# One-column products in place of transposes for the modulation turns, and four waits behind means taken out

## The reference

```
silu_c = jax.nn.silu(c)                                   # [1, 2048]
mod_l = jnp.split(silu_c @ w_mod[l] + b_mod[l], 6, axis=-1)   # w_mod [2048, 12288]
hl  = modulate(rms_norm(xl, norm1_g[l]), mod_l[0], mod_l[1])
xl  = xl + mod_l[2][:, None, :] * mixer_output(...)
hl2 = modulate(rms_norm(xl, norm2_g[l]), mod_l[3], mod_l[4])
xl  = xl + mod_l[5][:, None, :] * sq_relu_ffn(hl2, ...)

# layer_norm, in the gated branch (sgu) and in the convolution branch
xc  = xf - jnp.mean(xf, axis=-1, keepdims=True)
var = jnp.mean(xc * xc, axis=-1, keepdims=True)
```

## Time and profile before

| | |
|---|---|
| median of 3 runs | 2732.12 us (2731.7 to 2733.49) |
| the profiled execution | 2731.7 us, span 2729.9 us |
| TensorE matmuls | 2675.9 us busy, 21400 |
| TensorE weight loads | 2556.2 us busy, 21400 |
| VectorE | 1914.7 us busy, 2949 instructions |
| ScalarE | 1268.8 us busy, 1836 instructions |
| DMA | 539.02 MB, mean 197 GB/s |

### The profile page before, as it was taken

One profiled execution on the slowest core, in us unless ns is written; L12 is line 12 of the kernel. 1 busy time (PEld: TensorE's weight loads), 2 busy tenths in 40 slices (PEclk: granted clock), 3 DMA queues, 4 the chain that ended last, 5 costly groups with the idle time before them and its releaser, 6 DMA issues.

```text
span 2729.9 us, 51382 instructions
## 1 busy us (share of the span) xinstructions
PE 2675.9 (98%) x21400; PEld 2556.2 (94%) x21400; DVE 1914.7 (70%) x2949; ACT 1268.8 (46%) x1836; POOL 149.9 (5%) x162
## 2 busy tenths in 40 slices
PE   7999999999999999999999999999999999989998
PEld 4599977899999999999999999999999999989997
DVE  5765789889897788886555555677656665478564
ACT  4622344454446445544443444464444444554453
POOL 0000011100014001100000000030000000100000
PEclk9999999999999999999999999999999999999999
DMA  7766755455555788887555565564434444535553
GB/s 302 300 226 232 236 179 180 143 200 186 186 187 185 250 287 276 268 279 245 185 187 189 182 195 189 188 195 151 159 132 155 154 147 147 174 125 190 184 194 131
DMA packets 163991, 539.02 MB, mean 197 GB/s; under 512 B 31024, under 2 KB 35120, under 8 KB 163632
## 3 DMA queue, kind: packets, MB, share of 16 engines
q1 hardware_dynamic: 163760, 535.73, 58.9%
HBM read 533.57 MB, written 2.10 MB: 196 GB/s over the span
## 4 chain that ended last, share of the span: by engine, by line
PE 88%; DVE 6%; DMA 3%; issue 1%; ACT 1%; SPq 1%; DVEq 0%; POOL 0%; ACTq 0%
PE ps L566 26%; PE ps L571 26%; PE ps L568 26%; DVE lo L1694 2%; DMA raw<-in_w_ff 2%; PE ps L782 1%; PE ps L801 1%; DMA raw<-in_w_mod 1%; PE ps L729 1%; PE ps L717 1%; PE ps L790 1%; ACT hi L1078 1%; DVE row L2269 1%; PE ps L959 0%; SPq L484 0%
## 5 line engine op out<-in xcount | busy, mean ns | idle before, releaser
L1078 ACT ACTIVATE hi<-raw 128x1024 fp32r<-128x1024 f32 x856 | 901.3, 1057 | 899.4 <-PE ps L571 477.1
L566 PE MATMUL ps<-AH,hi 128*128 128x256 f32 (+2 forms) x4432 | 1263.4, 285 | 2.8 <-DVE AL L2108 2.7
L571 PE MATMUL ps<-AH,lo 128*128 128x256 f32 (+2 forms) x4432 | 1252.0, 282 | 7.3 <-DVE lo L1694 7.3
L568 PE MATMUL ps<-AL,hi 128*128 128x256 f32 (+2 forms) x4432 | 1253.3, 283 | 0.0
L1694 DVE TENSOR_TENSOR lo<-raw,hi 128x1024 fp32r<-128x1024 f32 x856 | 1038.6, 1226 | 205.1 <-ACT hi L1078 203.6
L566 PEld LDWEIGHTS ps<-AH,hi 128*128 128x128 f32 x4432 | 837.4, 189 | 32.8 <-issue 29.1
L571 PEld LDWEIGHTS ps<-AH,lo 128*128 128x128 f32 x4432 | 836.2, 189 | 10.1 <-DVE lo L1694 10.0
L568 PEld LDWEIGHTS ps<-AL,hi 128*128 128x128 f32 x4432 | 835.4, 188 | 0.8
L571 PE MATMUL ps<-YH,lo 128*128 128x256 f32 (+1 forms) x1512 | 421.1, 279 | 0.6 <-DVE lo L1694 0.5
L566 PE MATMUL ps<-YH,hi 128*128 128x256 f32 (+1 forms) x1512 | 421.1, 279 | 0.0
L568 PE MATMUL ps<-YL,hi 128*128 128x256 f32 (+1 forms) x1512 | 421.1, 279 | 0.0
(11 more groups left out here) (277 smaller groups left out, 2491.5 us busy)
## 6 DMA issues: line engine op xcount, KB each, us to landing
raw<-in_w_ff SPq DMA_DIRECT2D x256, 512.0 KB, 4.2
raw<-in_w_in SPq DMA_DIRECT2D x208, 512.0 KB, 4.2
raw<-in_w_mod SPq DMA_DIRECT2D x192, 512.0 KB, 4.8
raw<-in_w_ain SPq DMA_DIRECT2D x128, 512.0 KB, 3.6
raw<-in_w_pin SPq DMA_DIRECT2D x64, 512.0 KB, 3.5
raw<-in_w_o SPq DMA_DIRECT2D x32, 512.0 KB, 4.7
raw<-in_w_aout SPq DMA_DIRECT2D x32, 512.0 KB, 3.5
raw<-in_w_pout SPq DMA_DIRECT2D x32, 512.0 KB, 3.5
```

The lines of the kernel that those rows point to most:

```text
L566: e.matmul(b.ap[:, o], hi[:, k, :], xh, start=start and k + i == 0, stop=False, skip_group_check=many)
L568: e.matmul(b.ap[:, o], hi[:, k, :], xl, start=False, stop=False, skip_group_check=many)
L571: mm = e.matmul(b.ap[:, o], los[j % NSPLIT][:, k, :], xh, start=False, stop=stop and k == KU - 1, skip_group_check=many)
L1078: e.activation(his[u % NSPLIT][:, :, :], raws[raw_at[i]][:, :].rearrange("p (k m) -> p k m", k=KU), ACT.Copy).then_inc(s_hi, 1)
```

## The change

Three edits. The turn on TensorE is four plain products in place of four transposes: the stationary operand is the same slice of `macc`, the moving operand is a column of ones (`one`, one number on each partition) in place of the 128x128 identity. So the sum over the partitions is made by the array, and each product writes one column of `XB`. On VectorE the sum over 512 columns goes, with the wait behind it, and the addition of the bias reads the four columns from `XB`. The tile `msum`, which had held the four sums, is no longer written or read; its place is kept under another name. In `norm_means`, both waits on `s_mean` go; the function runs twice (`sgv_m` and `sgv`, `cv_m` and `cv`), so TensorE has four waits less. No instruction changes its place among the others; the `yield`s are the same.

```
@@ TensorE, mod_turn
                 for j in range(4):
-                    mm = e.transpose(XB[:, 128 * j:128 * j + 128], macc[n % 2][:, 128 * j:128 * j + 128], ident)
+                    mm = e.matmul(XB[:, j:j + 1], macc[n % 2][:, 128 * j:128 * j + 128], one, start=True, stop=True)
                 mm.then_inc(s_modt, 1)
@@ TensorE, norm_means
                 mean(first, T, last=ADD[first] + 8)
-                e.wait_ge(s_mean, MEAN[first] + 1)
                 yield
...
                 mean(second, T, last=ADD[second] + 8)
-                e.wait_ge(s_mean, MEAN[second] + 1)
                 yield
@@ VectorE, mod_out
                 e.wait_ge(s_modt, MODS.index(nb) + 1)
-                e.reduce_sum(msum[:, 0:4], XB[:, :].rearrange("p (j t) -> p j t", j=4), AX.X).then_inc(*own.up())
-                done()
-                e.tensor_tensor(modv[:, 4 * nb:4 * nb + 4], msum[:, 0:4], cols("b_mod", 4, 4 * nb),
+                e.tensor_tensor(modv[:, 4 * nb:4 * nb + 4], XB[:, 0:4], cols("b_mod", 4, 4 * nb),
                                 ALU.add).then_inc(s_modv, 1)
@@ the tiles
-        msum = sb("msum", [128, 120], F32, ctx, "right")
+        sb("back", [128, 120], F32, ctx, "right")
```

## The result

| | before | after |
|---|---|---|
| median | 2727.9 us (2720.8 to 2733.5, 7 runs) | 2744.5 us (2738.5 to 2752.0, 7 runs) |
| ratio, 95% interval | | 1.0063 [1.0048, 1.0079] |
| profiled execution, span | 2731.7, 2729.9 us | 2743.35, 2741.5 us |

What follows compares the result with a forecast made beforehand. TensorE, busy 98% of the span, was taken as the bound. Terms 5.5 + 0 - 0.25 + 0.4 - 1.0 = +4.65 us, less 1.2 for the pitch, gave +3.5 to the median: 2735.6 us, range 2728 to 2741.

Steps and rivals of the forecast that it cites:

- TensorE's side of a turn: Each turn on TensorE: eight weight loads instead of four, 0.93 us against 0.44, taken as +0.50 us a turn.
- the earlier trace: Upper bound from the nearest complete turn, near 141.62 us, with 4 array rows and two columns: +0.73 us a turn.
- four passes for a plain product: Rival: each plain product in a turn takes four passes, 1.8 us a turn, 2746 us in all; chance 0.03.
- Turns under cover: Turns near which TensorE waits anyway (308, 1123, last three): the extra 0.5 us is wholly or partly hidden.
- 308 and 1129: Turn at 308 hidden, 0; turn at 1123, ahead of TensorE's 2.68 us wait for VectorE, -0.25 us.
- all three last ones: Turns at 1167, 1205 and 1243, where the weight ring is nearly full: stops absorb part, +0.4 us together.
- VectorE and the waits: VectorE loses 10.4 us, credited only at 1123 and the ring; three dropped waits give -1.0 us, the fourth 0.
- my eleven: Eleven turns with TensorE working without a wait around them, three in attention: 11 x 0.50 = +5.5 us.
- a term that I can't size: TensorE's pitch, 117 or 112 ns, drawn again at each interruption; leaning to the faster, put in as -1.2 us.
- the third: Rival: turns cost 0.73 us and ring stops absorb nothing, or a fast stretch becomes slow; 2741 us, chance 0.24.
- the faster rival: Rival: two or more long stretches fall to 112 ns after the interruptions at 518 to 855; 2725 us, chance 0.15.

Runs made afterwards that it cites:

- t1: The changed kernel's one-column turns and addition from PSUM, with the four waits behind the means kept; 2740.8 us, 1.0038 against the kernel before.
- v3: The changed kernel itself, run and traced a second time; 2745.4 us, 1.0057 against the kernel before.
- x1: The changed kernel (one column) with an idle 4-row product at 646 us and behind the last convolution mean; 2739.2 us, 1.0041 against the kernel before.
- u4: The changed kernel with an unread reduction of 512 numbers put back on VectorE in each turn; 2743.3 us, 1.0060 against the kernel before.
- t2: The kernel before with only the four waits on the means taken out; 2729.9 us, 1.0004.
- v4: The kernel before with ten idle 4-row products: two at 646 and 856 us, eight behind the last eight turns; 2729.9 us, 0.9996.
- x2: The changed kernel with 128 equal columns of ones and idle 4-row products at two places, run again; 2729.9 us, 1.0001 against the kernel before.
- v1: The kernel before with an idle 4-row product at two places, 646 and 856 us; 2726.9 us, 0.9992.
- w3: The changed kernel with 128 equal columns of ones and idle 4-row products at two places, first run; 2726.0 us, 0.9996 against the kernel before.
- u2: The kernel before with one idle 128-column identity product at about 650 us; 2726.4 us, 0.9991.

## Why the prediction was wrong, by its steps

**TensorE's side of a turn (0.50): right.** Two records a product, eight a turn, 0.46 by the distance of starts (1.13 for 0.67 or 0.68 us), in every turn outside attention that has weight matmuls on both sides. The price of the 128x1 records in the kernel before carried over; the earlier trace rows were the wrong neighbour. The Trainium skill (TensorE: Matmul & The Clock Gate, Terms) has transpose mode as 4 times faster for FP32. Read as four passes for a plain product, that gave my estimate of 1.8 us a turn. The trace doesn't bear it out: it has half as many records as that takes, and 1.13 us from the last weight matmul ahead to the second one behind.

**Turns under cover: right for 308 and 1129**, 0.01 and a wait 0.84 shorter (turn included, -0.4 for -0.25 forecast). In attention the three turns cost 0.35, not 0.50. The turns at 1167 and 1205 had no cover and cost 0.46 each, where I had given all three last ones +0.4; together about +1.0. These two misses (-0.8 and +0.6) nearly cancel, which is luck. In the two profiled executions the whole of 1138 to 1246 us came out at -0.1; over four one-column traces without added work (changed, t1, v3, x1) it lies 0.7 above the mean of five with transposes.

**VectorE and the waits: right in kind.** The relief counts at the two places named and nowhere else that is seen, with about 2 us in u4's trace, more than I gave it; the time doesn't show it. Three waits gave about 0.3 each in the trace, and alone they can't be measured (t2).

So the sum is 11 x 0.46 (eight of my eleven, with 1123, 1167 and 1205) + 3 x 0.35 + 0.1 at the last turn - 0.84 - 1.0 = +4.4; I had +4.65.

**The step that failed is "a term that I can't size".** I took the pitch of a stretch for a draw that every interruption makes anew, independent of what the interruption is, and so gave it -1.2 us, leaning to the faster. Both halves were wrong. What stands in the turn has a say: behind one-column products the four stretches are slow in 20 of 20 (five executions), whatever comes in, and with the four early turns it is 40 of 40. Behind transposes 14 of 24 are fast (six executions, v4 with its further products among them). For the stretches behind the turns the sign was therefore positive and could not lean the other way. The size, against 128 columns with a fast entry, is 9.4 us (x1, x2), twice what I had worked out for everything else. Against before, which has two of the four slow anyway, the four stretches give 2 x 1.6 = 3.2, the one at 190 us 1.0, and the last up to 2.6, while the stretches from 250 to 318 us give 1.0 back.

With it: 4.4 + 3.2 + 1.0 - 1.0 + 1.6 (2.6 in three of five kernels) = 9.2 of the 17 us. With the 1.0 of the waits put back it is 10.2, and t1, which keeps them, measured 10 (5 to 15). The rest of the changed kernel, 8 us (4 to 12), is not placed. A candidate is the long stretch from 646 to 838 us, worth 7.6: of 19 runs of one-column kernels without waits and idle products (changed, v3, u4) only four lie below 2739 us, as if it were slow more often than before, of whose runs beside the experiments 41 of 130 lie above 2732. x1 speaks for it in part: the idle products, with both stretches ahead of the turns fast, bring the changed kernel from 1.0063 and 1.0057 to 1.0041, some 5 us, where the same products bring the kernel before 2 (v1). These differences lie within their intervals. And a run without a profile doesn't show its stretches; of the three profiled ones one had the long stretch fast. Why it should be slow more often stays open.

**The rivals.** The one that came nearest is the third, for the part of it that said a fast stretch becomes slow; but I had priced it as a single stretch beside a dearer turn, with a chance of 0.24. My reason against the faster rival, that the draw is nearly the same every time because three runs agreed within 1.8 us, was worth little: 7 runs of before span 13 us. I had seen the two values, and should have asked which stretches stand behind a turn, since the change acts on those first. The kernel before had five of them, three fast: there was more to lose than to win.

**Better versions.** w3 and x2 keep the changed kernel's idea (no reduction, no waits) and win its loss back: 0.9996 [0.9987, 1.0004] and 1.0001 [0.9990, 1.0013]. Nothing tried is faster than the kernel before by more than the measurement tells; u2 at 0.9991 [0.9979, 1.0003] comes closest, by one idle product.

## What to carry to other kernels

Where a change puts other instructions between two stretches of equal work on the bound engine, count equal windows of those stretches before and after; here everything that could be counted was forecast to 0.3 us in the sum, in part by luck, and it is a quarter of the loss. In a plain float32 product each 128x128 stationary tile costs two loads, and fewer moving columns save none of it: a turn of transposes with a reduction on an engine that has time can be the cheaper one. When a kernel's runs fall in groups, look in the profile for the stretch whose price is the distance between them, before three runs that agree are taken for its spread.

## What was not expected of the hardware

- TensorE streams 256-column matmuls, each with its own weights, in one of two pitches at a granted clock of 1.00: 342 (117.8 ns) or 355 to 356 (113.3 ns) in 40 us; one stretch, at 2515 us, has 118.9 in all traces. A stretch keeps its value from one interruption to the next, 200 us long if need be. Stretches of 258 or 272 columns have one value of their own in all kernels, 120.3 and 125.2 ns.
- The instructions between two stretches act on the value. Eight records of one column left the slow one (40 turns of 40, five executions), eight of 128 equal columns kept it (32 of 32, both ways), eight of 32 columns turned it over (8 of 8, one execution), four transposes left either. Why was not found; "few rows" and "the last product" were tried and fell.
- An idle product at 646 us was followed by the fast value in all six kernels that had it, against six of fourteen without; one behind the mean at 854 us in five of five, against four of fifteen.
- Eight plain records take 1.01 us from the first of them to the second weight matmul behind, with 1, 32 or 128 moving columns; four transposes take 0.56. The columns don't set it; each record comes with a weight load of its own.
